# Decoder step: one more column pair by seven block products, and sample rows halved once at the end

## The reference, cut to what matters

```
h = rms_norm(x, ln2_pre) * (1 + sc2) + sh2
f = jnp.square(jax.nn.relu(h @ w_ff1)) @ w_ff2      # 1024 -> 4096 -> 1024
x = x + g2 * rms_norm(f, ln2_post)
```

## Time and profile before

| | us |
|---|---|
| median of 3 runs | 835.02 |
| the profiled execution, its own time | 836.17 |
| its span (first to last instruction) | 834.5 |
| TensorE busy with matmuls | 786.7 (94%) |
| VectorE busy | 508.2 (61%) |
| ScalarE busy | 378.3 (45%) |
| feed-forward part: first matmul after its last start-up wait, to the end | 440.9 to 834.5 |

### The profile page before, as it was taken

The page is one execution under the profiler, slowest core; times in us unless marked ns, Lnnn a source line. Parts: engine busy times, 40 slices in busy tenths (PEclk is TensorE's granted clock), DMA queues, the critical chain, the costliest instruction groups (busy, mean ns, idle before and its releaser), DMA issues.

```text
span 834.5 us, 12954 instructions
## 1 busy us (share of the span) xinstructions
PE 786.7 (94%) x4728; PEld 631.7 (76%) x4728; DVE 508.2 (61%) x1012; ACT 378.3 (45%) x760; POOL 113.9 (14%) x160
## 2 busy tenths in 40 slices
PE   6899989999989989799989999999999999999997
PEld 2577567788745666568769988899888998899885
DVE  0532777999768975434656752397246954388465
ACT  4544533234356754323664532377124762168431
POOL 2034302349523330010000000000000000000000
PEclk9999999999988999999999999999999999999999
DMA  8924520313349889753323123033311341132603
GB/s 308 365 79 130 172 69 0 113 51 102 102 150 330 267 298 354 253 199 121 107 101 102 63 89 101 10 128 116 101 51 51 102 151 52 51 102 101 214 1 114
DMA packets 70370, 112.14 MB, mean 134 GB/s; under 512 B 7506, under 2 KB 32670, under 8 KB 70170
## 3 DMA queue, kind: packets, MB, share of 16 engines
q1 hardware_dynamic: 64194, 96.34, 34.4%
q0 software_dynamic: 4224, 10.37, 3.8%
q10 hardware_dynamic: 1888, 4.59, 1.5%
HBM read 103.88 MB, written 9.09 MB: 135 GB/s over the span
## 4 chain that ended last, share of the span: by engine, by line
PE 82%; DVE 6%; DMA 5%; ACT 3%; issue 2%; SPq 1%; DVEq 0%; POOL 0%; ACTq 0%
PE bank L889 79%; PE bank L892 3%; DMA raw<-in_ada_w 3%; DMA pages<-in_cache_k 1%; DVE w_split L2039 1%; DMA raw<-in_w_in 1%; ACT w_split L1537 1%; SPq L683 1%; DVE w_split L602 1%; DVE keys L2039 0%; ACT stage L1562 0%; ACT h_raw L1562 0%; DVE act_lo L2039 0%; DVE tok_lo L2039 0%; DVE probs L2303 0%
## 5 line engine op out<-in xcount | busy, mean ns | idle before, releaser
L889 PE MATMUL bank<-w_split,hid_hi 128*128 128x512 f32 x512 | 158.9, 392 | 0.0
L889 PE MATMUL bank<-tok_hi,w_split 128*128 128x288 f32 x640 | 135.4, 298 | 9.0 <-DVE stage L2508 5.0
L889 PEld LDWEIGHTS bank<-tok_hi,w_split 128*128 128x128 f32 x640 | 105.5, 189 | 11.1 <-DVE w_split L2039 5.6
L889 PEld LDWEIGHTS bank<-w_split,hid_hi 128*128 128x128 f32 x512 | 96.0, 188 | 20.7
L889 PE MATMUL bank<-act_hi,w_split 128*128 128x512 f32 (+1 forms) x288 | 101.0, 409 | 1.9 <-DVE act_lo L2039 1.8
L889 PE MATMUL bank<-w_split,hid_lo 128*128 128x512 f32 x256 | 100.1, 391 | 0.0
L889 PE MATMUL bank<-tok_lo,w_split 128*128 128x288 f32 x320 | 94.7, 296 | 0.0
L2039 DVE TENSOR_TENSOR w_split<-raw,w_split 128x512 fp32r<-128x512 f32 x84 | 55.7, 686 | 50.2 <-ACT w_split L1562 49.5
L1562 ACT ACTIVATE w_split<-raw 128x512 fp32r<-128x512 f32 x84 | 50.2, 622 | 69.8 <-PE bank L889 69.6
L602 DVE TENSOR_TENSOR w_split<-raw,w_split 128x2048 fp32r<-128x2048 f32 (+2 forms) x21 | 46.6, 2219 | 39.3 <-ACT w_split L1537 39.1
L889 PEld LDWEIGHTS bank<-act_hi,w_split 128*128 128x128 f32 (+1 forms) x288 | 53.7, 186 | 21.3 <-issue 7.1
(11 more groups left out here) (279 smaller groups left out, 1427.8 us busy)
## 6 DMA issues: line engine op xcount, KB each, us to landing
raw<-in_w_ff SPq DMA_DIRECT2D x32, 1024.0 KB, 5.4
raw<-in_ada_w SPq DMA_DIRECT2D x18, 1024.0 KB, 5.8
raw<-in_w_in SPq DMA_DIRECT2D x10, 1024.0 KB, 5.6
pages<-in_ada_w SPq DMA_DIRECT2D x6, 1024.0 KB, 8.0
pages<-in_cache_k SPq DMA_DIRECT2D x24, 256.0 KB, 5.9
v_pages<-in_cache_v SPq DMA_DIRECT2D x24, 256.0 KB, 5.4
raw<-in_w_out SPq DMA_DIRECT2D x4, 1024.0 KB, 7.4
x_in<-in_x_prompt SPq DMA_DIRECT2D x1, 2048.0 KB, 10.3
```

The source lines that it names most:

```text
L889: return nc.tensor.matmul(out, lhsT, rhs, start=start, stop=stop, skip_group_check=True)
```

## The change

Pair 3 is computed with seven block products, as pairs 4 to 15 are. That is 84 matmuls in place of 96. Its weight, and all pieces of the second weight, are therefore split by units. ScalarE's and VectorE's streams for pairs 0 to 2 are written out anew, with the work that pair 3 needs put between them: four weight sums of pair 3, the mixed tokens, their splits, five units. The token mixes, which before were done by the end of pair 3, stand mostly ahead of it. In pairs 4, 8 and 12 VectorE's order is changed: the weight sums of the next pair stand behind the additions of P67 and P5 and of P4. The sample rows are summed as 128 rows over the rounds, and the lower 64 are added to the upper ones once for each `nh` after the last round.

The core of the diff (the banks and the rooms follow from the first two hunks):

```diff
-BY_UNITS = SPLIT[NTH[AT[("w1", 4)]]:]
+BY_UNITS = SPLIT[NTH[AT[("w1", 3)]]:]
...
-            if f == 0:
+            if p < 3:
                 for u in range(4):
                     take(("w1", 2 * i + u // 2, u % 2), (4 * i + u) % 3)
...
-                if p >= 4:
+                if p >= 3:
                     for product in PRODUCTS:
                         product_steps(product, p)
```

ScalarE's stream up to pair 3, where `first_outputs(n)` is what the two loops of before did for the hidden block n (on ScalarE relu and the high parts, on VectorE the square and the low parts):

```diff
+            first_outputs(0)
+            first_outputs(1)
+            hi_until(AT[("w1", 2)] + 1)
+            first_outputs(2)
+            run(mix1_hi[:, :, :], h_raw[:, 0:4, 1, :]).then_inc(S["mix_hi"], 1)
+            first_outputs(3)
+            run(mix2_hi[:, :, :], h_raw[:, 4:8, 1, :]).then_inc(S["mix_hi"], 1)
+            hi_units(4)
+            first_outputs(4)
+            run(mix3_hi[:, :, :], h_raw[:, 0:4, 0, :]).then_inc(S["mix_hi"], 1)
+            first_outputs(5)
+            run(tok_hi[:, 0:4, 1, :], h_raw[:, 4:8, 0, :]).then_inc(S["mix_hi"], 1)
+            hi_units(1)
```

ScalarE, `pair_outputs(p)`:

```diff
+                later = p % 4 and p > 3
+                if later:
                     hi_units(1)
-                if p > 4:
+                if p > 3:
                     evacuated(act, ("P67", p - 1))
                 free(run(p1_kept[:, :], full(act, ("P1", p))[:, 0:HN]), ("P1", p))
-                if p % 4:
+                if later:
                     evacuated(act, ("P53", p - 1))
                     hidden_hi(2 * p - 2, 2 * p)
                 else:
                     hi_units(3)
-                hi_units(2)
+                if later:
+                    hi_units(2)
                 act.wait_ge(S["w1_done"], 2 * p)
                 act.wait_ge(S["w1s_done"], 2 * p)
                 free(run(stage_tok[:, 0, 0, :], full(act, ("C11", p))[:, 0:HN]), ("C11", p))
                 evacuated(act, ("C11", p))
-                hi_units(4)
+                if not later:
+                    hi_units(2)
+                hi_units(1 if p == 3 else 4)
                 evacuated(act, ("P4", p))
                 hidden_hi(2 * p + 1, 2 * p + 1)
```

VectorE's stream up to pair 3:

```diff
+            first_outputs(0)
+            first_outputs(1)
+            lo_until(AT[("w1", 2)] + 1)
+            gates(1)
+            mixed(quarter_raw(0, 1), quarter_raw(0, 1), quarter_raw(0, 0))
+            first_outputs(2)
+            mixed(quarter_raw(1, 1), quarter_raw(1, 1), quarter_raw(0, 1))
+            weight_sums(3, (1, 2))
+            first_outputs(3)
+            weight_sums(3, (3, 4))
+            mixed(quarter_raw(0, 0), quarter_raw(1, 1), quarter_raw(0, 0))
+            minus(mix1_lo[:, :, :], quarter_raw(0, 1), mix1_hi[:, :, :]).then_inc(S["mix_lo"], 1)
+            first_outputs(4)
+            mixed(quarter_raw(1, 0), quarter_raw(1, 0), quarter_raw(1, 1))
+            minus(mix2_lo[:, :, :], quarter_raw(1, 1), mix2_hi[:, :, :]).then_inc(S["mix_lo"], 1)
+            lo_units(4)
+            minus(mix3_lo[:, :, :], quarter_raw(0, 0), mix3_hi[:, :, :]).then_inc(S["mix_lo"], 1)
+            first_outputs(5)
+            lo_units(1)
```

VectorE, after each half of rounds 1 to 3:

```diff
-                        for t in range(NT):
+                        for t in range(NT + 1):
                             free(nc.vector.tensor_tensor(out_t[:, t, s], full(dve, ("w2", f, nh, t))[:, :], out_t[:, t, s],
                                                          ALU.add), ("w2", f, nh, t))
-                    dve.wait_ge(S["low_rows"], 3 + 2 * f + nh)
-                    y = out_t[0:TS, NT, s]
-                    if f:
-                        link(nc.vector.tensor_tensor(y, y, half_s[:, :], ALU.add))
-                        free(nc.vector.tensor_tensor(y, full(dve, ("w2", f, nh, NT))[0:TS, :], y, ALU.add), ("w2", f, nh, NT))
```

VectorE, once for each `nh` at the end, behind ScalarE's copy of the lower rows of `out_t` to `half_s`:

```diff
+            def add_low_rows(nh):
+
+                dve.wait_ge(S["low_rows"], 3 + nh)
+                y = out_t[0:TS, NT, 512 * nh:512 * nh + 512]
+                nc.vector.tensor_tensor(y, y, half_s[:, :], ALU.add).then_inc(S["rows_summed"], 1)
+                dve.wait_ge(S["rows_summed"], nh + 1)
```

More of the change, by code:

```diff
@@ L1186, in by_token @@
                 for half in range(2):
-                    if kind == "w2" and first >= 4:
+                    if kind == "w2":
                         parts = [unit_parts(("w2", first + half, c)) for c in range(4)]
@@ L1200, in by_token @@
                             k = 4 * half + k4
[L1201 removed]
+                            if kind == "w2" and t == 0:
                                 pe.wait_ge(S["unit_lo"], UNIT_NO["w2", first + half, k4])
@@ L1466, in product_steps @@
                 x_hi, x_lo = unit_tokens(product)
-                if p == 4 and product in MIXED:
+                if p == 3 and product in MIXED:
                     pe.wait_ge(S["mix_lo"], MIXED[product])
@@ L1605, in hi_units @@
                     if key[0] in ("P5", "P6", "P67", "P53"):
-                        act.wait_ge(S["summed"], 4 * (key[1] - 4) + {"P5": 1, "P6": 2, "P67": 3, "P53": 4}[key[0]])
+                        act.wait_ge(S["summed"], 4 * (key[1] - 3) + {"P5": 1, "P6": 2, "P67": 3, "P53": 4}[key[0]])
                     run(unit_parts(key)[0], unit_source(key)).then_inc(S["unit_hi"], 1)
@@ L1898, in _, with keep_low_rows @@
                     hi_until(AT[("wo", 0)] + 1)
-            def keep_tokens(kind, f, nh, copy, low, last_piece):
-                for t in range(NT):
[L1904 to L1911, removed]
+            def keep_low_rows():
+                run(half_s[:, :], full(act, ("wo", 0, NT))[TS:2 * TS, :]).then_inc(S["low_rows"], 1)
+                hi_until(AT[("wo", 1)] + 3)
             hi_until(AT[("wo", 0)] + 3)
@@ L1940, in _ @@
             hi_until(AT[("wo", 3)] + 3)
[L1943 to L1964, removed]
@@ new lines, in first_outputs @@
+            def first_outputs(n):
+                st = stage_tok[:, n % 2, :, :]
+                if n >= 2:
+                    act.wait_ge(S["w1_done"], n - 1)
+                    act.wait_ge(S["w1s_done"], n - 1)
+                for x in range(2):
+                    free(run(st[:, x, :], full(act, ("w1", n, x))[:, 0:HN], ACT.Relu), ("w1", n, x))
+                act.wait_ge(S["w1_squared"], n + 1)
+                run(hid_hi[:, n % 8, :].rearrange("p (x t) -> p x t", x=2), st[:, :, 0:HP]).then_inc(S["w1_hi"], 1)
+                run(hid_s[:, n % 8, 0:TS].rearrange("p (x t) -> p x t", x=2), st[:, :, HP:HN]).then_inc(S["w1s_hi"], 1)
@@ L2537, in pair_outputs @@
                 add(stage_tok[:, 1, 1, :], "P5", p, u3_kept[:, :])
+                if not later and sums:
+                    weight_sums(p + 1, (2, 3))
                 lo_units(1)
                 add(stage_tok[:, 1, 0, :], "P4", p, u3_kept[:, :])
-                lo_units(2)
+                lo_units(1)
+                if not later and sums:
+                    weight_sums(p + 1, (4,))
+                if not later and p > 3:
+                    lo_units(3)
+                lo_units(1)
                 evacuated(dve, ("C11", p))
```

160 lines of the change are left out of this document (71 added, 89 removed).

## The result

The changed kernel takes **845.25 us** (median of 4 runs, 841.07 to 846.02) against 834.23 us (4 runs, 832.67 to 836.53) of the kernel before beside it: ratio 1.0104, 95% interval 1.0075 to 1.0133. It is slower by 1%, where 841.9 had been forecast. The profiled execution took 845.14 us with a span of 843.5, that of before 836.17 with 834.5: 9.0 us to be found. The medians lie 11.0 us apart, since the profiled execution of before was 1.9 us slower than its median and that of after 0.1 faster; those 2 us lie between executions, and no profile shows where.

The account below looks back on a forecast made before the run. TensorE was taken to bound the kernel. Pair 3 +2.9, later rounds +2.4 and clock +1.6 gave +6.9 us: 843.1 for the profiled execution, 841.9 as median after the 1.15 offset; range 837.0 to 845.5.

Parts of the forecast that it names:

- the waits for `p_kept` and `w_split` in pair 3: Expected TensorE gaps: about 3.2 us for ScalarE's `p1_kept` near 478, 1.3 us for VectorE's `w_split` near 471.
- P67's 0.8: In pairs 5, 9 and 13, TensorE was to idle 0.8 us before P67, waiting for P6's addition on VectorE.
- the half clock from 479: In pair 3, TensorE's clock was expected at half for some 3 us from 479.
- pauses ahead of pair 3: VectorE was to run without a pause from 450 to 478; pauses there would show the forecast wrong.
- Pair 3, +2.9 forecast: Pair 3: idle 1.3 us before P1 and 3.2 before C11, less 1.6 for the saved product: +2.9 us.
- Rival D: VectorE meets P1's and C11's needs in time and the three later gaps clear: 828.4 us, chance 0.08.
- Pairs 4, 8 and 12, +0.8 a round forecast: Gaps of 1.7 us at C11 and 0.8 at P67 replace 1.68 at P53: +0.8 a round, +2.4 us in all.
- the forecast's zero: In pairs 4, 8 and 12, the time at which TensorE could begin P53; offsets count from it.
- The term of the sum that was mis-sized: Clock falls to half once, after pair 3's 3.2 us gap: 1.6 us; gaps of 1.7 and 0.8 cost 0.
- Rival C: Clock falls in pairs 5, 9 and 13 too: up to 4.8 us more, 846.7 us, chance 0.06.
- Sample rows, 0 forecast: Additions and copies dropped in rounds 1 to 3, about 1.4 us put before the end: 0 us, all covered.
- The rule on banks: Pair 3's bank reuse: by the rule alone, three claims show at worst 0.5 us each, 1.5 for the pair.

Follow-up runs that it names:

- the second: The changed kernel profiled once more, unchanged, against the kernel before: 844.09 us (8 runs), ratio 1.0088.
- The front-end reordering: The changed kernel with ScalarE's and VectorE's streams up to and in pair 3 queued anew, later pairs kept: 838.47 us, ratio 1.0033 to before.
- the kernel with both orders: The changed kernel with ScalarE's and VectorE's streams queued anew both up to pair 3 and in pairs 4 to 15: 828.10 us, ratio 0.9905 to before.
- the order alone in the kernel before: The kernel before with only the changed streams of pairs 4, 8 and 12, pair 3 keeping eight products: 838.81 us, ratio 1.0046.
- the idle matmuls: The changed kernel with two unused matmuls issued ahead of C11 in pairs 5, 9 and 13: 844.10 us, ratio 1.0104 to before.
- the old order: The changed kernel with the streams of pairs 4, 8 and 12 as before, pair 3 at seven products: 841.56 us, ratio 1.0065 to before.
- the sample rows: The kernel before with only the sample rows kept as 128 and halved once at the end: 834.62 us, ratio 0.998.

## Why the prediction was right, and where a size was off

The time lay in the range, close under its upper end of 845.5, with the sign forecast, and the queues and waits that were named are the ones that cost. Where the clock would fall was not foreseen, and that the total still lay in the range owes something to luck: what the clock took stands in other places than the sum has it. Of the signs that the forecast set itself, the waits for `p_kept` and `w_split` in pair 3 came, P53 of pair 4 waited no more, and C11 of pairs 5, 9 and 13 waited. P67's 0.8 and the half clock from 479 did not come in the first profile; 0.46 and the half clock came in the second. Idle time, worked out near 12 us, was 10.1 in the first and 11.5 in the second. And VectorE did have pauses ahead of pair 3, four of 0.76 to 0.77 us between 456 and 478; the forecast's own working contained them, so the sign contradicts that working. Step by step:

- **Pair 3, +2.9 forecast, +3.27 measured.** Gaps of 1.3 and 3.2 us were forecast, 1.23 and 3.05 came. P1's unit was put at 471.6 and began at 471.94, the square of block 5 was put to end at 476.0 and did so near 476.4 (475.62 + 0.75), the copy's end was forecast for 478.7 and came at 479.05. The forecast added and subtracted idle times by their length; with 0.24 more for each, 1.23 + 3.05 + 0.48 - 1.49 is the 3.27 measured. The front-end reordering took both gaps away and the saved product appeared (94.32 against 95.81: 1.49, forecast 1.6). VectorE's pauses of 0.77 inside a block's round were in the pitch of 2.27 that the sum used; that they could be filled by other work was the part not seen. Rival D was weighed as if VectorE's instructions had to be shorter; they only had to stand in another order. Its number, 828.4, is about what the kernel with both orders then took, 828.10, beside 836.90 of before on that chip.
- **Pairs 4, 8 and 12, +0.8 a round forecast, +0.9 measured** with the clock kept (98.65 against 97.71), both by the order alone in the kernel before and in after with the idle matmuls. Where P5's addition began (546.73, forecast as -1.4) puts the forecast's zero at 548.1: the copy was due at +6.4, 554.5, and ended at 554.74. Gaps of 1.7 and 0.8 were forecast (its own terms give 1.6 and 0.9, with the same sum), 1.93 and 0.46 came: 2.4 together, against 2.5. Two gaps in place of one pay the 0.24 twice, which is why the round is 0.9 longer although the idle time grew by only 0.7.
- **The term of the sum that was mis-sized is the clock**: "1.6, since 3.2 is beyond the gap that did cost it, once", and for the gaps of 1.7 "nearer to 1.68: 0". In the first profile it was kept after 3.05 us and lost after each 1.93: 2.8 us. In the second it was lost at 3.08, for 2.6 us, and kept three times. Rival C had falls in pairs 5, 9 and 13, beside that of pair 3 and at 1.6 each, with a chance of 0.06; they came without pair 3's and at 0.9 each. A fall cost 0.8 to 2.6 us here, and the forecast's single number was a value of something that differs between executions of one program. The spread of after's runs, 841.07 to 846.83, is of about the size of the clock's cost, and in the eight later runs the longest has the lowest mean clock (846.83 at 0.977) and the shortest the highest (841.49 at 0.984). Where in the kernel the unprofiled runs lost it is not shown.
- **Sample rows, 0 forecast, 0 measured** (ratio 0.998 with 1 in its interval). The last tile's addition after the change still waited the same 1.94 us for TensorE as in the earlier trace rows (VectorE in after):

```profile
837.46 0.69 DVE L2610 TENSOR_TENSOR out_t<-bank,out_t 128x512 f32<-128x512 f32 x1 [1.94 <-PE bank L889]
```

- **The rule on banks.** The Trainium skill's page "Perfetto Trace Analysis", section "Matmuls", wants independent groups rotated through PSUM banks. The kernel with both orders reuses P1's and P6's banks at the same distance as after and shows no gap over 0.2 us behind the start-up of the feed-forward part. As forecast, what is queued ahead of the copy decided, not the distance.

The whole: forecast +6.9 on the span, measured +9.0, of which 0.35 lies ahead of the changed code, 0.4 is pair 3, and 1.2 the clock (2.8 against 1.6); the rest, 0.2, is in the rounds. The median lay 3.3 over the forecast: 2.0 of it by the profiled execution, and 1.3 since after's median did not lie 1.15 below its profiled execution, as had been taken over from before. The saved product (1.49) and the three waits removed (1.68 + 0.24 each) were worth 7.3 us together. More than that was given back as new waits for the same two engines, and all of it was there to be had: the four stretches with both orders sum to 380.05 against 387.56 before, 7.5 us less. Those of after sum to 396.18, 16.1 more than with both orders, and that is made up of 4.75 us of waits in pair 3, 2.86 in each of the three rounds (98.65 against 95.79 with the clock kept; each gap with its 0.24), and 2.8 for the clock.

What stays open: which idle times lose the clock. The gap's length alone doesn't tell: 1.68 lost it in none of the nine cases in the profiles of before, of the old order and of the sample rows, 1.93 in 6 of 15, 2.37 to 2.43 in three of four, and 3.05 to 3.08 in two of six. Open is also why one execution took 2719.39 us.

## What to carry to other kernels

A product saved on the bounding engine is worth its time only if what the side engines owe that engine still arrives in order; price the place in the queue of every copy that frees a bank, and not the length of the copy. Count the number of idle times as well as their sum. When one instruction is late behind a queue, don't move that one alone: the lateness of the queue shows up one product later. Lay the whole stream anew, with ready work behind each instruction that another engine must answer, and give the clock a range of its own wherever a change brings TensorE a new idle time.

## What the hardware showed that was not expected

The granted clock of one unchanged program fell in different places in two profiles, at gaps equal to 0.03 us: 1.00 after 3.05 and half after 1.93 in the one, the reverse in the other. By the rows of 2 us it was at half for some 3.4 us after a gap of 1.93, and for some 6.8 us at that of 3.08, from 478.9 to 485.7. A slow clock also hides a wait: P67's 0.46 is absent just where the clock fell, so the loss to be named is the difference of the rounds, 0.9 on average, and not the 1.7 by which the matmuls themselves were slower.
